# Router with stationary weights in four column groups, and expert 0 gathered transposed

## What is computed

```python
logits = (ht @ w_router + b_router)             # 256 x 1024 @ 1024 x 32
top_val, top_idx = lax.top_k(logits, TOP_K)     # 4 of 32 experts a token
wts = jax.nn.softmax(top_val, axis=-1)
# for each expert e, on the rows that chose it:
a = clamped_swiglu(xb @ w_up[e] + b_up[e])      # 1024 x 2048
y = a @ w_down[e] + b_down[e]                   # 1024 x 1024
# weighted sum of y back to the tokens, residual, final rmsnorm
```

## Time and profile before

| | |
|---|---|
| Median of 3 runs | 1081.66 us (1081.4 to 1081.82) |
| Span of the profiled execution | 1078.8 us; 2.9 us of the median lie around it |
| TensorE busy | 1028.3 us (95%) |
| DMA moved | 423.34 MB, 392 GB/s over the span |
| End of attention, start of expert 0's up products | 145.1 and 171.45 us |

### The profile page before, as it was taken

The page is one execution under the profiler, slowest core; times in us unless marked ns, Lnnn a source line. Parts: engine busy times, 40 slices in busy tenths (PEclk is TensorE's granted clock), DMA queues, the critical chain, the costliest instruction groups (busy, mean ns, idle before and its releaser), DMA issues.

```text
span 1078.8 us, 12673 instructions
## 1 busy us (share of the span) xinstructions
PE 1028.3 (95%) x5097; PEld 409.9 (38%) x5097; DVE 223.3 (21%) x637; ACT 155.0 (14%) x388; POOL 20.6 (2%) x49
## 2 busy tenths in 40 slices
PE   7899999999999999999999999999999999999996
PEld 5686654333333333333333333333333333333332
DVE  3344433111111111111111111111112101111112
ACT  2323332011000011111111111111101100111102
POOL 4001000000000000000000000000000000000000
PEclk9999999999999999999999999999999999999999
DMA  9982469999999999999999999999999999999994
GB/s 281 315 313 93 157 252 378 399 405 426 429 426 433 433 431 430 432 431 432 430 433 429 435 431 433 431 429 435 431 431 431 430 433 424 428 427 427 428 426 201
DMA packets 36827, 423.34 MB, mean 392 GB/s; under 512 B 8226, under 2 KB 12370, under 8 KB 18996
## 3 DMA queue, kind: packets, MB, share of 16 engines
q1 hardware_dynamic: 36644, 422.37, 93.8%
q10 hardware_dynamic: 144, 0.39, 0.1%
HBM read 421.70 MB, written 1.05 MB: 392 GB/s over the span
## 4 chain that ended last, share of the span: by engine, by line
PE 77%; DMA 18%; DVE 3%; ACT 1%; issue 1%; DVEq 0%; SPq 0%
PE ps L1129 31%; DMA ring<-in_w_up_dram 18%; PE ps L1162 17%; PE ps L1174 5%; PE ps L1084 4%; PE ps L916 4%; PE ps L994 3%; PE ps L923 2%; PE ps L1109 2%; PE ps L945 1%; DVE work L1604 1%; PE ps L1099 1%; DVE work L1648 1%; PE ps L1142 1%; PE ps L1021 1%; PE ps L1033 1%
## 5 line engine op out<-in xcount | busy, mean ns | idle before, releaser
L1129 PE MATMUL ps<-ring,work 128*64 128x512 f32 x2040 | 447.2, 594 | 8.3 <-DMA ring<-in_w_up_dram 8.2
L1129 PEld LDWEIGHTS ps<-ring,work 128*64 128x64 f32 x2040 | 142.8, 137 | 309.7 <-issue 290.9
L1162 PE MATMUL ps<-ring,work 128*64 128x512 f32 x1008 | 223.3, 595 | 21.1 <-DVE work L1648 21.1
L1613 DVE TENSOR_SCALAR work<-ps 128x512 f32<-128x512 f32 x31 | 21.4, 691 | 641.4 <-PE ps L1129 641.4
L1162 PEld LDWEIGHTS ps<-ring,work 128*64 128x64 f32 x1008 | 69.8, 137 | 154.4 <-issue 129.0
L811 ACT ACTIVATE work<-work 128x512 f32<-128x512 f32 x31 | 19.5, 630 | 453.1 <-DVE work L1613 453.1
L1174 PE MATMUL ps<-work 64*128 64x512 f32 x256 | 63.6, 615 | 0.7 <-ACT work L823 0.7
L1084 PE MATMUL ps<-xt,work 128*64 128x512 f32 x256 | 60.6, 593 | 0.2 <-DVE work L1562 0.2
L823 ACT ACTIVATE work<-ps 128x512 f32<-128x512 f32 x32 | 19.1, 597 | 236.6 <-PE ps L1162 236.6
L916 PE MATMUL ps<-ring 128*128 128x256 f32 x192 | 42.5, 380 | 0.0
L916 PEld LDWEIGHTS ps<-ring 128*128 128x128 f32 x192 | 36.0, 190 | 5.0 <-issue 0.4
(11 more groups left out here) (245 smaller groups left out, 521.3 us busy)
## 6 DMA issues: line engine op xcount, KB each, us to landing
ring<-in_w_up_dram SPq DMA_DIRECT2D x40, 4096.0 KB, 35.1
ring<-in_w_up_dram SPq DMA_DIRECT2D x44, 2048.0 KB, 16.6
ring<-in_w_down_dram SPq DMA_DIRECT2D x20, 4096.0 KB, 35.0
ring<-in_w_down_dram SPq DMA_DIRECT2D x21, 2048.0 KB, 14.8
ring<-in_w_in_dram SPq DMA_DIRECT2D x8, 1024.0 KB, 8.5
ring<-in_w_up_dram SPq DMA_DIRECT2D x7, 1024.0 KB, 12.0
ring<-in_w_out_dram SPq DMA_DIRECT2D x4, 1024.0 KB, 10.0
ring<-in_w_down_dram SPq DMA_DIRECT2D x4, 1024.0 KB, 29.1
```

The lines of the kernel that those rows point to most:

```text
L1129: t = pe.matmul(UP[h * 64:h * 64 + 64, a, :], xgT[:, k, :], row[:, a * 64:(a + 1) * 64, h, :], start=False, stop=(k == KD - 1), skip_group ...
L1162: t = pe.matmul(ps[h * 64:(h + 1) * 64, XG, :], aT[:, j, u * 64:u * 64 + 64], w[:, j * D + h * 512:j * D + (h + 1) * 512], start=(u == 0 a ...
L1613: dve.tensor_scalar(t1, up_pairs[:, 0], 7.0, None, ALU.min).then_inc(swi, 1)
```

## The change

The router is swapped: `wr` (32 columns) is now stationary and `x2T` moves, and the eight pieces are spread over four groups of 32 array columns, so that partitions 32g to 32g+31 of PSUM hold a partial sum. ACT copies them to `lgT` (`read_groups`), and one matmul with four stacked identities (`eye4`) adds and turns them (`sum_groups`). Tile 1's first half is multiplied before the position matmuls.

Expert 0's gather is swapped too: `xt` is stationary and `pm` moves, which gives the rows already transposed. ACT's copy and the four transposes of expert 0 are gone, DVE copies each half to `xgT`. As pieces now hold 128 adjacent rows, expert 0's up weights are read in another row order (`first_v`). `up` begins when the first half is in `xgT`; the bias of expert 0 is added after its first four pieces. `keep_warm` is gone.

```diff
+        lgT = dump[1][:, 0:2 * P].rearrange("p (n q) -> p n q", n=NT)
+        first_v = w_up[0, 0].rearrange("(u j p) f -> u p j f", j=2, p=P)
...
             def square_part(j, part, n, lo, hi):
-                if j == 3:
-                    act.wait_ge(squared[0], 3 + part)
+                act.wait_ge(squared[0], 2 * j - 2 + part)
...
+            def read_groups(n):
+                act.wait_ge(groups_done, n + 1)
+                act.activation(lgT[:, n, :], ps[:, LOGITS[n], P:2 * P], ACT.Copy).then_inc(groups_read, 1)
...
+            read_groups(0)
             read_x2T(1, 0, 4, PJ[0], 7)
...
             read_x2T(1, 6, 8, PJ[0], 9)
+            read_groups(1)
             take_root(3)
...
-            read_xg(0)
             select(1, 1)
...
-            def route(n, ks, ready):
+            def route_groups(n, ks, ready):
                 pe.wait_ge(x2T_ready, ready)
                 for k in ks:
-                    t = pe.matmul(ps[:, LOGITS[n], 0:E], x2T[:, k, n * P:(n + 1) * P], wr[:, k, :],
-                                  start=(k == 0), stop=(k == KD - 1), skip_group_check=True)
+                    g = k % 4
+                    t = pe.matmul(ps[g * E:(g + 1) * E, LOGITS[n], P:2 * P], wr[:, k, :], x2T[:, k, n * P:(n + 1) * P],
+                                  start=(k < 4), stop=(k >= 4), skip_group_check=True)
...
+            def sum_groups(n):
+                pe.wait_ge(groups_read, n + 1)
+                pe.matmul(ps[:, LOGITS[n], 0:E], lgT[:, n, :], eye4, start=True, stop=True,
+                          skip_group_check=True).then_inc(logits_done, 1)
+            def first_gather(n, half):
+                for k in range(4 * half, 4 * half + 4):
+                    t = pe.matmul(ps[:, (XTB, XG)[half], k % 4 * TOK:(k % 4 + 1) * TOK], xt[:, n, k * P:(k + 1) * P],
+                                  pm[:, n, :], start=(n == 0 and k % 4 == 0), stop=(n == 1), skip_group_check=True)
...
                 for u in range(UP_UNITS):
+                    if first and u == 2:
+                        up_bias(b, prev, first=True)
+                        pe.wait_ge(xgT_read, b + 1)
...
             pe.wait_ge(pm0_ready, 1)
-            gather_tile(0)
+            first_gather(0, 0)
             pe.wait_ge(m_ready, 2)
             pe.matmul(ps[:, PLACES[1], 0:E], upper[:], M[:, 1, :], start=False, stop=True).then_inc(pos_done, 1)
-            keep_warm(2)
+            first_gather(0, 1)
             pe.wait_ge(pm_ready, 1)
-            gather_tile(1).then_inc(xg_done, 1)
-            up_bias(0, False)
-            gather_turn(0)
-            keep_warm(3)
-            up(0, False, in_singles(0), biased=True, halves=True)
+            first_gather(1, 0).then_inc(first_gathered, 1)
+            first_gather(1, 1).then_inc(xg_done, 1)
+            up(0, False, in_singles(0), first=True)
...
+            def read_first(half, done, ready):
+                dve.wait_ge(done, 1)
+                k = slice(4 * half, 4 * half + 4)
+                dve.tensor_tensor(xgT[:, k, :], ps[:, (XTB, XG)[half], 0:4 * TOK].rearrange("p (k t) -> p k t", k=4),
+                                  gfT[:, k].unsqueeze(2).broadcast_to([P, 4, TOK]), ALU.mult).then_inc(ready, 1)
```

More of the change, by code:

```diff
@@ L206, in hybrid_layer @@
         sel = carve(64)
-        eye2 = carve(32)
+        eye4 = carve(32)
         pcol = carve(2)
@@ L463, in _, with load_unit @@
                     load_win(c, half, lo, 512, 0)
-            def load_unit(e, u, place, loaded):
+            def load_unit(e, u, place, loaded, first=False):
                 part = slice(u % 2 * UNIT, u % 2 * UNIT + UNIT)
-                if u < UP_UNITS:
+                if first and u < UP_UNITS:
+                    sp.dma_start(place.rearrange("p (j f) -> p j f", j=2), first_v[u]).then_inc(loaded, 16)
+                elif u < UP_UNITS:
                     sp.dma_start(place, up_v[ds(e, 1), u // 2].rearrange("a p f -> p (a f)")[:, part])\
@@ L763, in _ @@
             act.activation(root[:, 5:6], ident[:, 0:1], ACT.Sqrt)
[L764 to L768, removed]
+            for a in range(4):
+                act.activation(eye4[a * E:a * E + E, :], ident[a * E:a * E + E, a * E:a * E + E], ACT.Copy)\
+                   .then_inc(eye4_ready, 1)
+            act.wait_ge(eye4_ready, 4)
+            act.activation(sel[0:2 * E], eye4[0:2 * E, 0:1].broadcast_to([2 * E, TOK]), ACT.Copy).then_inc(sel_ready, 1)
             def square_part(j, part, n, lo, hi):
-                if j == 3:
-                    act.wait_ge(squared[0], 3 + part)
-                act.activation(dump[part][:, 0:hi - lo], xt[:, n, lo:hi], ACT.Square, accum_out=sq_sum[:, j, part:part + 1])\
+                act.wait_ge(squared[0], 2 * j - 2 + part)
+                act.activation(dump[0][:, 0:hi - lo], xt[:, n, lo:hi], ACT.Square, accum_out=sq_sum[:, j, part:part + 1])\
                    .then_inc(squared[0], 1)
@@ L1092, in gather @@
                 for n in range(NT):
-                    t = gather_tile(n)
+                    for h in range(2):
+                        t = pe.matmul(ps[h * 64:(h + 1) * 64, XG, :], pm[:, n, :], xt[:, n, h * 512:(h + 1) * 512],
+                                      start=(n == 0), stop=(n == 1), skip_group_check=True)
                 t.then_inc(xg_done, 1)
             def gather_turn(b):
-                pe.wait_ge(xg_read, b + 1)
+                pe.wait_ge(xg_read, b)
                 for j in range(4):
@@ L1106, in up_bias @@
                     pe.wait_ge(aT_read, b * 2)
+                if first:
+                    pe.wait_ge(bup_in, 32)
                 for a in range(2):
@@ L1110, in up_bias, with up @@
                                       bup[a * E:a * E + E, :].rearrange("e (p h x) -> e p h x", h=2, x=8)[:, :, h, :],
[L1111 removed]
+                                      start=not first, stop=False, skip_group_check=True)
                 t.then_inc(bias_used, 1)
[L1114 to L1116 removed]
+            def up(b, prev, unit, last=False, first=False):
+                if first:
+                    pe.wait_ge(first_xgT, 1)
+                else:
                     up_bias(b, prev)
[L1118 removed]
+                    pe.wait_ge(xgT_read, b + 1)
                 for u in range(UP_UNITS):
+                    if first and u == 2:
+                        up_bias(b, prev, first=True)
+                        pe.wait_ge(xgT_read, b + 1)
                     w = unit(u)
@@ L1124, in up @@
                             pe.wait_ge(last_half_in[u], 16)
-                        row = aside if halves and k == 1 else w[:, j * 2 * F:(j + 1) * 2 * F]
+                        row = aside if first and k == 1 else w[:, j * 2 * F:(j + 1) * 2 * F]
                         row = row.rearrange("k (p h x) -> k p h x", h=2, x=8)
@@ L1130, in up @@
                                               row[:, a * 64:(a + 1) * 64, h, :],
-                                              start=False, stop=(k == KD - 1), skip_group_check=True)
+                                              start=(first and k == 0), stop=(k == KD - 1), skip_group_check=True)
                             if last and k == KD - 1 and a == 0:
                                 t.then_inc(half_up, 1)
-                        if halves and k in (0, 2):
+                        if first and k in (0, 2):
                             t.then_inc(first_half_used, 1)
```

47 lines of the change are left out of this document (22 added, 25 removed).

## The result

The changed kernel takes 1084.13 us (median, 1082.96 to 1086.35), the kernel before 1081.56 (1080.47 to 1082.44): ratio 1.0027 [1.0019, 1.0035]. The forecast was 1079.5. The profiled execution took 1084.68 with a span of 1082.6, so 2.1 lie around it.

The account below looks back on a forecast made before the run. From 228 on the stream of weights was taken to set the end, fixed by TensorE's time at 224.50. Router 1.24 plus gather 2.01 less bias 1.02 gave 2.2 us less than 1081.66: 1079.5, range 1079.0 to 1080.1, wider 1078.7 to 1081.6.

Parts of the forecast that it names:

- the chance given to the clock: Rival: without `keep_warm` the clock falls at 163.5 and costs 4.8 us in all, 1084.2; chance 0.07.
- The router's term: Routers of tiles 0 and 1: DVE begins on tile 1's logits at 163.98 instead of 165.22, 1.24 us earlier.
- the four groups run side by side: Tile 0's router: eight whole-array matmuls of 1.8 us become 0.55 in four column groups.
- The gather's term: From selection matrix to expert 0's up products: 1.91 us instead of 3.92, 2.01 less.
- The up products with the bias inside: Expert 0's bias, before in a wait, now stands inside the up products and costs 1.02 us.
- The rival with its loads hidden: New gather's loads hidden, eight matmuls in 0.9 us, not 1.79: 3.1 less in all, 1078.6; chance 0.07.
- the column groups would then be serial: Rival in the router: tile 0 stays at 1.8 us, 0.2 less in all, 1081.5; chance 0.12.
- What bounds the end: The kernel's end is TensorE's time at 224.50 plus a fixed amount of weights.
- the last hole: DMA rate drop to 148 GB/s in 224 to 225, ended by TensorE freeing the place; no hole after it.
- the forecast from the sum: Router 1.24 plus gather 2.01 less bias 1.02: 2.2 us less, 1079.5; chance 0.66 for 1.6 to 2.7 less.
- The hole at 173: DMA rate drop to 82 GB/s in 173 to 174; a sign, expected smaller or gone after the change.

Follow-up runs that it names:

- before_cold: The kernel before without its five matmuls with unused results, nothing else changed; 1083.98 us, ratio 1.0019.
- gather_warm: The changed kernel with the old router and three matmuls with unused results ahead of the wait for `m_ready`; 1082.05 us, ratio 1.0008.
- after_warm: The changed kernel with four matmuls with unused results put back into TensorE's two waits; 1080.01 us, ratio 0.9986.
- the two delay kernels: The kernel before with three more 512-column matmuls, behind expert 0's down products (1084.7 us) or behind those of expert 4 (1082.55 us).
- bias_early: The changed kernel with all of tile 0's gather and expert 0's bias moved into TensorE's two waits, no unused matmuls; 1081.0 us, ratio 0.9996.
- router_only: The kernel before with the new router alone; old gather, bias and `keep_warm` stay; 1081.91 us, ratio 1.0003.

## Why the prediction was wrong

**The step that failed** is the chance given to the clock, 0.07. The prediction worked that case out: 1084.2, and the median is 1084.13. It put the fall at 163.5 and its price at 4.8 (gathers 2.7, router 0.3, up 1.75); it came at about 169.1 and cost 0.68, nothing and 2.63. So that the median met 1084.2 was partly luck: the clock took 1.5 less and the router gave 0.9 less than that case had. In TensorE's time the account closes: forecast 2.23 less, in the trace 2.23 more, and the 4.46 between them are the clock's 3.31, 0.92 of the router, 0.15 of the gather and 0.08 of the up products. The reason given for the low chance was that "no row here shows it falling with TensorE at work". But every row read was of a kernel that had five dummies in just these waits, and the 1.22 us of idle in 165 to 170 at clock 1.00 was with them. That row could say nothing of the same place without them; before_cold shows it falling there. (The other row for it was misread by a little: TensorE's last matmul before ends at 1071.3 and the clock falls at 1075.7, which is 4.5 us and not over 5.) The rule of the Trainium skill that the prediction cited (TensorE: Matmul & The Clock Gate, Part 1), that the low clock is the default and activity lifts it, agrees with the falls in the changed kernel and in before_cold, and pointed the right way; gather_warm, where it fell with PE's busy time at 2.00 of 2.00, shows that it isn't told from the busy time alone.

**The router's term** was mis-sized: 0.32 for 1.24. That the four groups run side by side was right: sixteen records in 0.57, where 0.55 was taken. The price had come from the bias's matmuls, read as quarters of the array; in the trace of before their loads are 32 x 64, an eighth each, so that 0.51 lay so near 0.57 is in part luck. The 0.92 went to three places. By the last projection piece 0.31 was gone: its loads start at 160.07, less 0.71 is 159.36, for 159.05 (in the matmuls' own starts, 160.26 and 160.35, it is 0.23). Two gaps of PEld where the shape changes lie ahead of it, 0.33 and 0.20. Another 0.25 fell up to the sum (164.72 less 0.71 is 164.01, for 163.45), with three more such gaps of 0.17 to 0.20; that the gaps cost just this is an inference. The last 0.36: the read of the logits came 0.89 after the sum's start (165.61 - 164.72) for 0.53: 0.41 of it is an "issue" between TensorE's signal and DVE that this instruction had before too. "0.1 to DVE" was taken from the position matmul, a row of another instruction; the chain of before had the right one, at 164.80 for 0.41.

**The gather's term** was right where the clock held, 1.86 for 2.01: from the read of the logits to up it is 6.23 before (165.22 to 171.45) and 4.37 in after_warm (164.93 to 169.30). The up products with the bias inside take 1.10 more than before (184.35 - 169.30 against 13.95) for 1.02. In after_warm the last 24 loads take 2.71 (2.69 forecast), and up begins directly behind them; the position matmul ahead of them takes 0.41, where 0.22 was taken. The rival with its loads hidden did not come. The first half of up starts before the second is in `xgT`, with no wait between them: 7.02, then the bias 1.02, as in the sum.

**The page on weight loads.** The Trainium skill (TensorE: Matmul & The Clock Gate, Part 3) says that a weight load overlaps with running matmuls only where the row groups differ. That the column groups would then be serial, with 1.8 for tile 0's router, was the prediction's inference from it. The trace speaks against both: the sixteen matmul records take 0.57, and their sixteen loads, which all span the array's 128 rows, lie at 158.81 to 159.19 while those matmuls run from 158.88 to 159.45. Here the measurement decides.

**What bounds the end** was right: TensorE's time at the last hole plus a fixed amount of weights, within 0.6 us in 13 of 14 profiles that lie up to 6.8 apart. That 2.77 us put ahead of the hole cost 3.0, and behind it 0.85 or nothing, is shown by the two delay kernels. With the clock held, the forecast from the sum, less the 0.92 of the router, is 1.3 below before; after_warm measured 1.6 and 1.3 below, and 1.1 in TensorE's time. A gain of 2.0 in TensorE's time (bias_early) brought 0.7 to 1.0 in the medians, which the relation doesn't explain. The hole at 173, which was to be smaller or gone, is still there in the changed kernel (123 GB/s in 174 to 176) and gone in after_warm:

```profile
173.00:174.00 1.00, 1.00 (x6) 0.29 (x4) 0.00 (x0) 0.00 (x0) 0.00 (x0) 1.00 1.02 426
174.00:175.00 1.00, 1.00 (x8) 0.42 (x6) 0.00 (x0) 0.00 (x0) 0.00 (x0) 1.00 1.02 426
```

**Verdict on the parts.** Router: 0.33 in the trace, nothing that the times can show. Gather and router together, with dummies in the waits: 1.3 to 1.6 us less than before, the only version that came out under the kernel before beyond its interval each time that it was measured. `keep_warm` left out of it: a loss of 4.1 by the medians and 3.3 in the traces, more than all the rest gives.

## What to carry to other kernels

A matmul whose result nobody uses is not idle weight: where a change takes it out, or empties a wait that it stood in, the clock's fall must be the first rival, priced from both levels and given a large chance, since the trace of a kernel that has the guard cannot show what happens without it. Where a stream of weights sets the end, find the last hole in the DMA rate: what TensorE lost ahead of it moved the end by about as much, and so did a gain of 1 us, while one of 2 us did not come out whole; what it lost behind it cost nothing in the trace. Compare kernels from a place behind the part that scatters, not from the span's start. Take the time from one engine's signal to another's start from the row of that very instruction, compare starts of loads with starts of loads, and count each change of the stationary operand's shape as a fraction of a microsecond, here 0.17 to 0.33.

## What was unexpected of the chip

The clock fell with no idle time of TensorE in the profile (gather_warm, 2.00 of 2.00 in 164 to 168, clock 0.68 in 166 to 168); from 163.28 to the fall at about 166.7 its records there had 32 to 128 moving columns. And it held in router_only with TensorE busy for 1.42, 1.34 and 1.69 of 2.00 us. It stayed at 0.50 through the gathers and came back during the up products of 512 columns: in the changed kernel they begin at 170.66 and it is at 1.00 from about 175.9, in gather_warm from 173.69 and 1.00 from about 177.0. The same code can have it in one execution and not in another: the changed kernel's trace has 1.00 in 40 to 44, where gather_warm's, with the same attention part, has 0.61 and 0.54.

A change of the stationary operand between 128 x 32 and 128 x 128 left PEld idle for 0.17 to 0.33 us, with no releaser in the profile. And DVE's first read of the logits starts 0.41 after its sequencer is through with the wait, in both kernels, where the next such step, after the position matmul, takes 0.05; the cause is open.
